# Four experts to a 128-row tile of 32 slots each, a weight ring of three 4 MB units, sample tokens in column tiles, and loads issued earlier

## The reference

```python
h = rmsnorm(x); proj = h @ w_in            # D = 1024; q/k/v/z, beta/alpha, sliding-window q/k/v, two gates
o_a = gated DeltaNet(conv + SiLU, l2norm, chunked delta rule, gated RMSNorm)      # 8 heads of 128
o_b = sliding-window attention(window 128, 16 heads of 64, 2 kv heads, sinks, relative bias)
x = x + (sigmoid(gA) * o_a + sigmoid(gB) * o_b) @ w_out
h2 = rmsnorm(x)
group  = argmax(h2 @ w_rg + b_rg)          # top 1 of 8 groups
expert = top 2 of the 8 experts of that group
x = x + sum over the two of weight * (silu(h2 @ w_gate[e]) * (h2 @ w_up[e])) @ w_down[e]
y = rmsnorm(x)                             # returned with states and caches
```

## Time and profile before

| | us |
|---|---|
| median of 3 runs (1820.24 to 1826.62) | 1822.44 |
| the profiled execution's own time | 1823.06 |
| its span, first to last instruction | 1821.1 |

### The profile page before, as it was taken

One profiled execution on the slowest core, in us unless ns is written; L12 is line 12 of the kernel. 1 busy time (PEld: TensorE's weight loads), 2 busy tenths in 40 slices (PEclk: granted clock), 3 DMA queues, 4 the chain that ended last, 5 costly groups with the idle time before them and its releaser, 6 DMA issues.

```text
span 1821.1 us, 20925 instructions
## 1 busy us (share of the span) xinstructions
PE 1509.3 (83%) x6916; PEld 869.5 (48%) x6916; DVE 810.8 (45%) x1700; ACT 331.8 (18%) x887; POOL 199.6 (11%) x301
## 2 busy tenths in 40 slices
PE   6698998998999989999999879728877777787880
PEld 5456757556566575575665754323222222222220
DVE  1156376565673765656737632342221221221224
ACT  3112222122131221221212220101111110110112
POOL 2201110111011110110111100021000000000002
PEclk9889999899998998998989969958898898988995
DMA  7922011030110110301101232037999999999995
GB/s 158 245 57 52 25 48 35 24 82 24 47 35 24 48 35 24 82 24 47 35 24 24 104 114 84 25 140 278 423 421 423 421 422 423 421 422 422 422 408 182
DMA packets 130366, 307.66 MB, mean 169 GB/s; under 512 B 19708, under 2 KB 92374, under 8 KB 105366
## 3 DMA queue, kind: packets, MB, share of 16 engines
q1 hardware_dynamic: 116934, 263.06, 39.6%
q0 software_dynamic: 8800, 27.52, 4.2%
q10 hardware_dynamic: 4608, 16.78, 2.3%
HBM read 273.50 MB, written 34.83 MB: 169 GB/s over the span
## 4 chain that ended last, share of the span: by engine, by line
PE 62%; DMA 22%; DVE 6%; issue 4%; ACT 4%; SPq 2%; POOL 0%; ACTq 0%; DVEq 0%; POOLq 0%
DMA arena<-in_w_up 20%; PE PB L1049 14%; PE PB L1066 11%; PE PB L1383 7%; PE PB L1072 5%; PE PB L1055 4%; PE PB L1327 4%; PE PB L1183 2%; PE PB L1155 1%; PE PB L1012 1%; DVE arena L1541 1%; PE PB L1092 1%; PE PB L1258 1%; PE PB L1267 1%; PE PB L1021 1%
## 5 line engine op out<-in xcount | busy, mean ns | idle before, releaser
L1383 PE MATMUL PB<-arena 128*64 128x512 f32 x1024 | 269.6, 675 | 113.7 <-DMA arena<-in_w_up 109.8
L1049 PE MATMUL PB<-arena 128*128 128x512 f32 x512 | 258.5, 669 | 0.0
L1066 PE MATMUL PB<-arena 128*128 128x384 f32 (+1 forms) x640 | 213.6, 487 | 0.0
L1383 PEld LDWEIGHTS PB<-arena 128*64 128x64 f32 x1024 | 76.6, 154 | 281.2 <-issue 143.1
L1867 DVE TENSOR_SCALAR arena<-arena 128x256 f32<-128x256 f32 x32 | 9.4, 295 | 381.9 <-ACT arena L928 381.9
L1049 PEld LDWEIGHTS PB<-arena 128*128 128x128 f32 x512 | 109.4, 217 | 136.8 <-issue 136.5
L1072 PE MATMUL PB<-arena 128*128 128x128 f32 x1280 | 156.9, 277 | 2.4 <-ACT arena L815 2.4
L1072 PEld LDWEIGHTS PB<-arena 128*128 128x128 f32 x1280 | 149.2, 192 | 7.0 <-ACT arena L815 3.2
L1066 PEld LDWEIGHTS PB<-arena 128*128 128x128 f32 (+1 forms) x640 | 108.9, 174 | 88.3 <-issue 29.0
L877 ACT ACTIVATE arena<-PB 128x512 f32<-128x512 f32 (+3 forms) x116 | 60.0, 521 | 481.2 <-PE PB L1391 253.8
L1403 PE MATMUL PB<-arena 128*64 128x512 f32 x512 | 116.9, 598 | 1.1 <-ACT arena L877 1.1
(11 more groups left out here) (396 smaller groups left out, 1788.0 us busy)
## 6 DMA issues: line engine op xcount, KB each, us to landing
arena<-in_w_gate SPq DMA_DIRECT2D x64, 1024.0 KB, 19.4
arena<-in_w_up SPq DMA_DIRECT2D x64, 1024.0 KB, 21.5
arena<-in_w_down SPq DMA_DIRECT2D x64, 1024.0 KB, 25.3
arena<-in_w_in SPq DMA_DIRECT2D x56, 512.0 KB, 5.4
ye_d<-arena ACTq DMA_DIRECT2D x32, 512.0 KB, 8.2
ye_d<-mixed SPq DMA_DIRECT2D x2, 2048.0 KB, 15.6
Sb<-in_state_dn SPq DMA_DIRECT2D x8, 512.0 KB, 4.0
out<-Sb POOLq DMA_DIRECT2D x8, 512.0 KB, 3.9
```

What stands on the lines that cost most here:

```text
L1049: last = mm(PB[g][:, :], wch[:, c, g, :], hT[:, c, 0:TP], start=c == 0, stop=c == KC - 1)
L1066: last = mm(PB[5 + n % 2][0:R, 0:3 * P], hT[:, c, n * P:n * P + R], wrow[:, c, :, :].rearrange("p g k -> p (g k)"), start=c == 0, stop=c = ...
L1383: last = mm(gu_bank[a][half[k], :], xT[:, a, c, half[k]], wgu[a][:, k, :, c, :], start=c == 0, stop=c == KC - 1)
```

## The change

`CAP` goes from 64 to 32 slots and a tile holds four experts, so there are 16 tiles in the first round instead of 32, and four column tiles of 32 in L1383 and L1403. The overflow round takes 8 expert blocks at a time (two tiles), instead of 4. The table of overflow experts is built with experts' bounds against the partition number and one small matmul, instead of with 1x1024 VectorE operations, and the count of overflow blocks with three operations instead of eight. Weights go through three units of 4 MB: the first half of the rows of gate and up of four experts, the second half, and down. A unit is reloaded when TensorE is through with it. 12 of the 1 MB equivalents are loaded before the stage.

```diff
-    CAP = 64
-    OV = (2 * T - 2) // CAP
+    CAP = 32
+    OV = -(-((2 * T - 2) // CAP) // 8) * 8
...
-            with eng.Fori(0, OV // 4) as it:
-                with eng.If(it * 4 < more):
+            with eng.Fori(0, OV // 8) as it:
+                with eng.If(it * 8 < more):
...
+            def load_half(u, k, e):
+                for g, w in enumerate((w_gate, w_up)):
+                    sp.dma_start(halves[u][:, k, g, :, :],
+                                 w[ds(e), :, :].rearrange("a (p u c) f -> u p (a c) f", u=2, c=KC // 2)[u]).then_inc(gu_in[u], 16)
...
+            with sp.Fori(1, NQ) as j:
+                sp.wait_ge(s_g0_ps, j)
+                for k in range(4):
+                    load_half(0, k, j * 4 + k)
+                sp.wait_ge(s_gu_ps, 2 + j)
+                for k in range(4):
+                    load_half(1, k, j * 4 + k)
+                sp.wait_ge(s_dn_ps, 2 + j)
+                for k in range(4):
+                    load_down(k, j * 4 + k)
...
+            def gate_up(it, a):
+                j = it * 2 + a
+                pe.wait_ge(s_xt_done, 1 + j * 2 + 2)
+                for u in range(2):
+                    pe.wait_ge(gu_in[u], j * 128 + 128)
+                    for c in range(KC // 2):
+                        for k in range(4):
+                            last = mm(gu_bank[a][own[k], :], xT[:, a, u * (KC // 2) + c, own[k]], halves[u][:, k, :, c, :],
+                                      start=u == 0 and c == 0, stop=u == 1 and c == KC // 2 - 1)
+                    last.then_inc((s_g0_ps, s_gu_ps)[u], 1)
...
-            def overlapped(it, a, turn=True):
-                gate_up(*later(it, a, 1), 0, KC // 2)
+            def one_quad(it, a, turn=True):
+                gate_up(it, a)
+                if turn:
+                    turn_x(*later(it, a, 1))
                 turn_hid(it, a)
-                gate_up(*later(it, a, 1), KC // 2, KC)
-                if turn:
-                    turn_x(*later(it, a, 2))
                 down(it, a)
```

```diff
                 pe.wait_ge(s_wch_in, h * 64 + 64)
+                pe.wait_ge(s_wrow_in, h * 48 + 48)
                 pe.wait_ge(s_o_done, 1 + h * NT)
+                for c in range(KC):
+                    xs = hT[:, c, TP:T]
+                    wr_ = wrow[:, c, :, :].rearrange("p g k -> p (g k)")
+                    first, end = c == 0, c == KC - 1
+                    mm(PB[6][0:32, 0:192], xs, wr_[:, 0:192], start=first, stop=end)
+                    mm(PB[6][32:64, 0:192], xs, wr_[:, 192:384], start=first, stop=end)
+                    mm(PB[6][64:96, 0:256], xs, wch[:, c, 0:4:2, :], start=first, stop=end)
+                    last = mm(PB[6][96:128, 0:256], xs, wch[:, c, 1:4:2, :], start=first, stop=end)
+                last.then_inc(s_projs_ps, 1)
...
-                        for k in range(4):
-                            for c in range(KC):
-                                last = mm(PB[4][:, k * TS:(k + 1) * TS], wch[:, c, k, :], hT[:, c, TP:T], start=c == 0, stop=c == KC - 1)
+                        for k in range(2):
+                            last = tr(PB[4][:, 64 * k:64 * k + 64], srow[HD:P, k, :], ident[HD:P, HD:P])
...
-                rows(4)
...
-                gate_mul(4)
                 softmax(0)
+                powt(2)
```

```diff
-            sp.wait_ge(s_rel_done, 1)
-            sp.dma_start(rel_d, relr.unsqueeze(1).to_broadcast([SH, P, 384])).then_inc(s_rel_out, 16)
-            sp.wait_ge(s_rel_out, 16)
...
+            conv_rows(0)
+            channel_weights(0)
+            sp.wait_ge(s_kd_ps, 1)
+            sp.wait_ge(s_bk_ps, NT)
+            row_weights(0)
+            sp.wait_ge(s_stored, 1)
+            states(0)
+            sp.wait_ge(s_rel_out, 16)
+            sp.dma_start(bias, bass.AP(rel_d.tensor, 127, [[383, P], [P * 384, SH], [1, 256]])).then_inc(s_bias_in, 16)
...
-            for v in range(2):
-                if v == 0:
-                    pe.wait_ge(s_bk_done, NT)
-                for c in range(KC):
-                    w = wkd[:, c, v, :, :].rearrange("p u d -> p (u d)")
-                    mm(PB[4 + v][:, :], w, hT[:, c, 0:TP], start=c == 0, stop=c == KC - 1)
+            for c in range(KC):
+                mm(PB[5][:, 0:TS], wk(c), hT[:, c, TP:T], start=c == 0, stop=c == KC - 1)
+            for c in range(KC):
+                last = mm(PB[4][:, :], wk(c), hT[:, c, 0:TP], start=c == 0, stop=c == KC - 1)
```

More of the change, by code:

```diff
@@ L450, in program @@
         LV = 6
+        gate_rows = (NP, *range(NP))
+        gate_bank = (PB[6], PB[5])
         @block.sync
@@ L473, in _ @@
+            conv_rows(0)
[5 more added lines that the diff above has]
+            states(0)
             sp.wait_ge(s_rel_out, 16)
             sp.dma_start(bias, bass.AP(rel_d.tensor, 127, [[383, P], [P * 384, SH], [1, 256]])).then_inc(s_bias_in, 16)
-            for k in range(2):
-                sp.dma_start(ye_rows[:, NPAIR + k * NP:NPAIR + (k + 1) * NP, :], mixed[:, 0:NP, :]).then_inc(s_bias_in, 16)
@@ L479, in _ @@
-            sp.wait_ge(s_kd_ps, 2)
-            sp.wait_ge(s_bk_ps, NT)
-            with sp.Fori(0, H) as h:
+            sp.wait_ge(s_bias_in, 16)
+            for r in range(NQ, J, NP):
+                k = min(NP, J - r)
+                sp.dma_start(ye_rows[:, r:r + k, :], bias.rearrange("p (a r) k -> p a (r k)", a=NP)[:, 0:k, :]).then_inc(s_bias_in, 16)
+            with sp.Fori(1, H) as h:
                 sp.wait_ge(s_proj_ps, 1 + h * 4)
-                for g, c0 in enumerate((0, GATE_W, 2 * GATE_W, C_SQ)):
-                    sp.dma_start(wch[:, :, g, :], w_r[:, :, ds(h * P + c0, P)]).then_inc(s_wch_in, 16)
+                channel_weights(h)
@@ L555, in down_weights @@
[L555 to L574 removed]
+            for k in range(4):
+                load_down(k, k)
@@ new lines, in _ @@
+            with sp.Fori(1, NQ) as j:
[3 more added lines that the diff above has]
+                sp.wait_ge(s_gu_ps, 2 + j)
+                for k in range(4):
+                    load_half(1, k, j * 4 + k)
+                sp.wait_ge(s_dn_ps, 2 + j)
+                for k in range(4):
+                    load_down(k, j * 4 + k)
+            def load(it, a, more):
+                j = it * 2 + a
+                chosen = [sp.value_load(ovt[0:1, ds(more * 8 + (4 * a + k))], min_val=0, max_val=NE - 1) for k in range(4)]
+                sp.wait_ge(s_g0_ps, j)
+                for k in range(4):
+                    load_half(0, k, chosen[k])
+                sp.wait_ge(s_gu_ps, 2 + j)
+                for k in range(4):
+                    load_half(1, k, chosen[k])
+                sp.wait_ge(s_dn_ps, 2 + j)
+                for k in range(4):
+                    load_down(k, chosen[k])
@@ L968, in _ @@
             more = further_blocks(act, further)
-            turns = (more + 3) // 4
+            turns = (more + 7) // 8
             for a in range(2):
-                act.wait_ge(ye_out[a], 1 + turns * 16 + 16 * (NPAIR // 2))
+                act.wait_ge(ye_out[a], 1 + turns * 16 + 16 * (NQ // 2))
             act.sem_inc(s_tok_done, 1)
@@ L1188, in _ @@
                 square(1)
+                pe.wait_ge(s_rows_done, 1 + h * NT + NT)
+                tr(b6[0:TS, 224:352], ks_, ident[:, :])
+                tr(b6[0:TS, 352:480], co[:, 2, TP:T], ident[:, :]).then_inc(s_smp_ps, 1)
                 pe.wait_ge(s_gm_ready, h * 2 + 2)
+                pe.sem_inc(s_pe_passed, 1)
+                mm(b6[0:TS, 0:TS], sS[:, 8, 0:TS], s_gt[:, :], start=True, stop=True).then_inc(s_smp_ps, 1)
+                scores(0)
+                square(2)
                 pe.wait_ge(s_smp_done, h * 13 + 5)
@@ L1361, in _ @@
             last.then_inc(s_rk_ps, 1)
+            pe.wait_ge(s_e_dif, 3)
+            mm(PB[1][0:1, 0:OV], rsc[0:OV, 0, 14:15], ident[0:OV, 0:OV], start=True, stop=True).then_inc(s_rk_ps, 1)
             pe.wait_ge(s_route_done, 1)
-            half = (slice(0, CAP), slice(CAP, P))
+            own = [slice(CAP * k, CAP * (k + 1)) for k in range(4)]
             def turn_x(it, a):
@@ L1789, in _ @@
             step(cp(cnt, PB[0][:, NT * 64:(NT + 1) * 64]))
-            step(ts(ov, cnt, float(CAP), None, ALU.is_gt))
-            for k in range(2, T // CAP + 1):
-                step(stt(ov, cnt, float(CAP * k), ov, ALU.is_gt, ALU.add))
+            step(ts(ov, cnt, 1.0 / CAP, -0.5 - 0.5 / CAP, ALU.mult, ALU.add))
+            step(ts(ov, ov, 12582912.0, None, ALU.add))
+            step(ts(ov, ov, -12582912.0, 0.0, ALU.add, ALU.max))
             src, dst = ov, ova
```

366 lines of the change are left out of this document (175 added, 191 removed).

## The result

The changed kernel takes 1748.1 us (median of four runs, 1741.7 to 1751.0), the kernel before 1822.2 beside it: ratio 0.959, 95% interval 0.955 to 0.962. The forecast was 1731, the range 1700 to 1768. The profiled execution took 1741.7 us and is the fastest of the four; its span is 1739.8. Where an execution is over 1.5% slower than the fastest of its kernel, the ratios leave it out; that holds for two of the four of split_loads alone.

What follows compares the result with a forecast made beforehand. TensorE was taken to bound the kernel up to 1234 us, full DMA engines the expert stage. 1823.1 - 92 (heads) - 22 (prelude) - 1.3 (router) + 24 (experts) = 1731.8, forecast 1731 us, 80% range 1700 to 1768.

Steps and rivals of the forecast that it cites:

- Part 1: Sample block in each head: 64 instructions in four column tiles take 4.0 us; gain 6.2 us a head.
- the 12.3 of no concurrency: Bound for the sample block's time in us, should its column tiles not run side by side at all.
- The 1.9 us kept for a cold start: Head start after a wait: of 2.2 us extra in the first 16 projection instructions, 1.9 was kept in the sum.
- Part 2: In each head, rows(4) and its gate product's wait go: 5.3 us a head saved, bounds 3 and 7.4.
- The 1.5 us wait for the last gate product: In the heads' new order, TensorE waits some 1.5 us for gate_mul of the last prompt tile.
- Part 3: Prelude: smaller row tiles, k matmuls once, earlier row weights; first head near 67.5 us, 22 us saved, bounds 14 and 26.
- Part 4: Router: seven operations of 0.25 us and the one before become three, saving 1.3 us.
- Part 5: Expert stage: 18 tiles including an overflow round, 231.2 MB at 416 GB/s in 556 us; 24 us more.
- rival B: Expert stage: the overflow round isn't run, 26.2 MB and 62 us less, 1669 us; chance 5%.
- A: Expert stage: all 4 KB rows go at 25.1 GB/s an engine, 408 GB/s, 567 us, total 1742 us; chance 20%.
- C: Heads: VectorE takes the gain as row tiles wait for gate products; 3 us a head remain, 1799 us; chance 6%.
- D: Expert stage: four column tiles share no better than two, clock stays 1.2 GHz; 44 us a tile, 2057 us; chance 3%.

Runs made afterwards that it cites:

- split_loads: Changed kernel with gate/up units of whole 8 KB rows, each 1 MB load also cut in two over halves of the partitions: 2124 us, ratio 1.156.
- block_first: Changed kernel with each head's sample block moved ahead of the three conv-row transposes: 1716.9 us, ratio 0.944.
- few_columns: Kernel before the change, with 28 of the 32 32-column matmuls of the sample tokens' projection left out in each head: 1745.4 us.
- late_bias: Changed kernel with the 3 MB bias-table write issued only after head 0's row weights land: 1741.8 us, ratio 0.955.
- old_experts: Changed kernel with the earlier kernel's expert stage (capacity, buffers, loads, routing table, expert code): 1719.0 us, ratio 0.944.
- experiments 3 and 4: Changed kernel with gate/up units of whole 8 KB rows: 1733.5 us; changed kernel with two experts' halves per load, rows still 4 KB: 1743.3 us.
- short_last: One expert's matmuls in the overflow round's second tile, against a kernel with whole-row units, needed overflow loads only, sample block first, late bias write: 1686.0 us against 1682.8.

## Why the prediction was right, and by how much each step

**Part 1 (sample block, 6.2 a head): 7.4.** The stretch to the first row tile fell from 41.3 to 33.9. The block takes 5.1 us in head 3 for the 4.0 forecast and 3.6 where the clock holds, so four tiles do run side by side, and the 12.3 of no concurrency was far off. But that the 4.0 came so near is luck. The row of 62 ns an instruction has matmuls of 132 columns, at half the clock; the block's are 224 wide on average. The sum took neither into account, and the two nearly cancel: in block_first the 64 take 56 ns each at 1.00. The row's window in before:
```profile
1059.13:1061.12 1.99, 1.98 (x32) 1.38 (x32) 0.00 (x0) 0.00 (x0) 0.00 (x0) 0.50 0.05 11
```
The 1.9 us kept for a cold start came from head 0, which begins after 14 us of waiting; at the other borders the wait is 1.5 us. In after's head 3 the projections take 7.06 + 20.80 = 27.9 us, for 28.2 + 1.9 in the sum, and the slow clock falls on the block instead, for some 1.5 us. L1055 weighs more in heads 4 and 6 than in head 0, which was summed up: few_columns gives 9.9 us a head back for seven eighths of it, 7.4 of own time and the slow clock behind it, in head 4 from 579 to 592 us.

**Part 2 (rows(4), 5.3 a head): 4.6** (75.5 to 71.0). The 1.5 us wait for the last gate product that was to come is there in after's head 3: VectorE's L1557, 2.56 us from 460.50, and L1558 behind it release TensorE's L1217 at 463.44. Parts 1 and 2 together: 93.2 for 92, which is luck in part, two errors of opposite sign in the fastest execution; with heads of 881 us the gain is 84.

**Part 3 (prelude, 22): 18.3.** The k matmuls end at 59.0 as forecast (59.2). The row weights needed 12.3 us from the first issue, not 8.5: the shared DMA engines were named and left out of the value. Without the write beside them the loads take 8.0, and late_bias gives 3.2 us at TensorE back.

**Part 4 (router, 1.3): 4.4,** 3.4 of which go with before's expert code (old_experts). Which of the router's operations it is was not taken apart.

**Part 5 (experts, +24): +34.7.** The count was right: five blocks, one round, 18 tiles; leaving it out gives back 64 us, and rival B said 62. Two terms were too small. The rate: 4 KB rows were put at 25.3 GB/s an engine, the mean of two queues that carry other things; the weight rows go at 24.9 (experiments 3 and 4), 412.3 GB/s in all for 416: 231.2 MB take 561 and not 556 us. The end: from about 1689 us, when the traffic falls (377 GB/s from 1686 to 1688, 197 and 107 in the next two windows of 2 us), to the last down's end at 1699.5 there are 10.5 us, for 6.5 forecast. The last down load lands only at 1694.3 and releases the last down, which takes 5.2 us; the last gate and up (from 1684.4), its activation and the turns are done less than half a microsecond earlier, so two ends nearly meet there. Of the 10.7 us these two terms are 9; the start is some 2.5 us earlier and not 3.4, and the last 1 is within what cutting the stretches can tell.

**The rivals.** A's mechanism is what happened: 4 KB rows at 24.9, even below its 25.1. A's sum had put all 231 MB at 25.1; with the forecast's own 71 MB at 26.1 it would have given 412.5 GB/s and 560 us, which is what came. So the 66% on the forecast's rate came half true: the measured rate lies midway between its 416 and A's 408. The rule of the Trainium skill ("DMA: Bandwidth & Descriptors", iDMA fabric), 408.7 GB/s for 4 KB rows, was of the right sign and size: 412.3 here, for weights of which two thirds have such rows.
B: the round was run. C: after's row tiles do not wait for VectorE; only L1217 does, 1.5 us in each head. D: refuted by short_last and by the page of after, where the expert stage's matmuls are busy (196.7 + 92.0) / 18 = 16 us a tile; D had 44, the forecast 22:
```profile
L1415 PE MATMUL PB<-arena 128*32 128x512 f32 x1152 | 196.7, 846 | 202.0 <-DMA arena<-in_w_up 201.1
...
L1435 PE MATMUL PB<-arena 128*32 128x512 f32 x576 | 92.0, 797 | 13.5 <-DMA arena<-in_w_down 6.9
```
The rule of the Trainium skill ("TensorEngine Tiling (Array Packing)", Key Properties) that a change of mode drains TensorE is not seen as a gap: in block_first the chain goes from L1298 to the block and from the block's last matmul to L1076 without an idle piece.

## What to carry to other kernels

Where the DMA engines are full, look first at how many partitions a load covers and how long a row it carries, and cut a ring's units along whole rows; the DMA share won't tell you, only MB over share does. A capacity that halves the work but sends a few experts into a second round must be counted on the routing, block by block, and a round's end is a chain of its own once its bytes are gone. Where TensorE waits a microsecond or two at a loop's border, order independent work into the gap: the wait can cost twice, once itself and once in the clock behind it.

## What the runs showed of the hardware

- Behind an idle time of 1.5 us TensorE's granted clock fell to 0.50 (1.2 GHz) for 3.4 or 6.8 us at six of seven borders of heads and not at all at one (after, head 2); with no idle time it stayed at 1.00 (2.4 GHz) at all seven, over the same 32-column-tile matmuls (block_first).
- It also fell to 0.50 without any idle time, for 6.8 to 13.7 us in each of eight heads, in and behind a group of 64 matmuls of 32 columns over a 128x128 stationary block (before); with 56 of the 64 left out it did not (few_columns).
- Weight loads with 8 KB rows a partition ran at 26.1 GB/s an engine, with 4 KB rows at 24.9, with a DMA share of 1.01 and 1.02; half as many loads of twice the size moved that by 0.1.
- Loads over 64 partitions at a time ran at 255 GB/s beside 422 for the same rows over 128, with the same DMA share of 1.02.
- One 32-wide column tile alone took as long as four (5.97 us for 8 matmuls at a clock of 0.61, 5.30 for 32 at 0.69; 7.1 and 8.3 us for 32 and 128 at 1.00).
- A 3 MB write in 1536-byte pieces held the DMA engines 89% busy at 98 GB/s (after, 31 to 58 us), and loads issued beside its end took 12.3 us where they took 8.0 without it.
